# The rounded half of a split piece written by ScalarE from PSUM instead of by VectorE from SBUF

## What is computed

```
# first block (adaLN from a vector c, residuals scaled by alpha = 2 ** 0.25)
u  = layer_norm(x) * (1 + scale1) + shift1
m  = concat(retention_4_heads(u @ w_in), gated_linear_attention_4_heads(u @ w_in)) @ w_out
x  = layer_norm(alpha * x + gate1 * m, ln1_w, ln1_b)
u2 = layer_norm(x) * (1 + scale2) + shift2
x  = layer_norm(alpha * x + gate2 * (square(relu(u2 @ w_ff1)) @ w_ff2), ln2_w, ln2_b)
# second block (mem: 256 rows)
y  = concat(ssd(x @ w_in), s5(x @ w_in), rglru(x @ w_in)) @ w_out
h  = layer_norm(alpha * x + y, ln1_g, ln1_b)
h  = layer_norm(alpha * h + cross_attention(h, mem, wq, wk, wv, wo), ln2_g, ln2_b)
h  = layer_norm(alpha * h + square(relu(h @ w1)) @ w2, ln3_g, ln3_b)
```

## Time and profile before

| | |
|---|---|
| median of three runs | 3189.3 us |
| the three runs | 3180.47, 3189.3, 3190.94 us |
| the profiled execution | 3180.87 us, span 3178.8 us |
| busy: PE | 2748.9 us (86%) |
| busy: DVE | 1526.9 us (48%) |
| busy: ACT | 967.1 us (30%) |
| busy: POOL | 685.1 us (22%) |
| mean granted TensorE clock | 0.931 |

### The profile page before, as it was taken

How to read it: one execution, slowest core, us unless ns; L and a number is a source line. 1 busy time by engine, 2 the same in 40 slices (tenths; PEclk the granted TensorE clock), 3 DMA queues, 4 the chain that set the end, 5 groups by cost and what they waited for, 6 DMA issues and landing times.

```text
span 3178.8 us, 34257 instructions
## 1 busy us (share of the span) xinstructions
PE 2748.9 (86%) x13390; PEld 1408.0 (44%) x13390; DVE 1526.9 (48%) x2347; ACT 967.1 (30%) x1115; POOL 685.1 (22%) x210
## 2 busy tenths in 40 slices
PE   5999958785899999998868785568889999999996
PEld 3577635532444444444454432224444444444443
DVE  6146223357344444456555559965324832222225
ACT  2323212212322222224333253215332422223331
POOL 1211011110122222211522122412511621112224
PEclk8999978887899999999989898878899999999998
DMA  8222030020111111111021220011101021111111
GB/s 276 80 67 67 31 106 27 27 93 1 53 53 53 53 53 53 48 48 38 28 80 66 67 80 0 0 40 38 42 27 40 27 67 39 53 53 53 53 40 53
DMA packets 95643, 172.83 MB, mean 54 GB/s; under 512 B 5648, under 2 KB 37792, under 8 KB 94752
## 3 DMA queue, kind: packets, MB, share of 16 engines
q1 hardware_dynamic: 83232, 134.70, 13.1%
q10 hardware_dynamic: 12288, 36.46, 3.2%
HBM read 164.85 MB, written 6.29 MB: 54 GB/s over the span
## 4 chain that ended last, share of the span: by engine, by line
PE 64%; DVE 15%; DVEq 5%; ACT 4%; issue 4%; POOLq 3%; DMA 1%; PEld 1%; SPq 1%; ACTq 1%; PEldq 0%; POOL 0%
PE PS L585 19%; PE PS L586 19%; PE PS L587 19%; DVEq L1863 2%; DVE XT L1864 1%; ACT WS L1341 1%; PE PS L1274 1%; DVE Hf L1864 1%; DVE S L2552 1%; ACT WB L1340 1%; DVE S L2556 1%; PE PS L624 1%; PE PS L1247 1%; DVEq L2558 1%; DVE ST L1883 1%
## 5 line engine op out<-in xcount | busy, mean ns | idle before, releaser
L480 POOL TENSOR_TENSOR WB<-WS,WB 128x2048 f16<-128x2048 f32 x108 | 448.3, 4171 | 2134.8 <-ACT WS L1341 2134.3
L585 PE MATMUL PS<-XT,WB 128*128 128x512 f16 (+1 forms) x1584 | 605.1, 382 | 33.9 <-DVE Hf L1862 10.8
L586 PE MATMUL PS<-XT,WB 128*128 128x512 f16 (+1 forms) x1584 | 604.5, 382 | 0.0
L587 PE MATMUL PS<-XT,WB 128*128 128x512 f16 (+1 forms) x1584 | 604.2, 381 | 0.0
L585 PE MATMUL PS<-WB,Hf 128*128 128x512 f16 x1440 | 548.7, 381 | 30.8 <-DVE S L2186 9.8
L586 PE MATMUL PS<-WB,Hf 128*128 128x512 f16 x1440 | 548.5, 381 | 0.0
L587 PE MATMUL PS<-WB,Hf 128*128 128x512 f16 x1440 | 548.4, 381 | 0.0
L1862 DVE CAST Hf<-S 128x512 f16<-128x512 f32 x172 | 158.4, 921 | 548.0 <-ACT S L1564 430.9
L1340 ACT ACTIVATE WB<-WS 128x2048 f16<-128x2048 f32 (+3 forms) x118 | 212.5, 1800 | 583.3 <-PEq L594 551.3
L585 PEld LDWEIGHTS PS<-XT,WB 128*128 128x128 f16 (+1 forms) x1584 | 155.6, 98 | 232.9 <-issue 33.0
L2183 DVE SCALAR_TENSOR_TENSOR R<-PS,R 128x512 f32<-128x512 f32 x176 | 120.9, 691 | 263.5 <-PE PS L587 259.7
(11 more groups left out here) (341 smaller groups left out, 3046.5 us busy)
## 6 DMA issues: line engine op xcount, KB each, us to landing
WS<-in_w_ff SPq DMA_DIRECT2D x32, 1024.0 KB, 5.1
WS<-in_mlp_w SPq DMA_DIRECT2D x32, 1024.0 KB, 5.2
WS<-in_w_in SPq DMA_DIRECT2D x48, 256.0 KB, 4.5
Hf<-in_w_ada ACTq DMA_DIRECT2D x12, 1024.0 KB, 7.6
Hf<-in_w_ada SPq DMA_DIRECT2D x8, 1024.0 KB, 10.2
WS<-in_w_out SPq DMA_DIRECT2D x8, 1024.0 KB, 5.0
WS<-in_w_in SPq DMA_DIRECT2D x14, 512.0 KB, 3.9
R<-in_x SPq DMA_DIRECT2D x4, 1024.0 KB, 10.1
```

The costliest lines, as they stand in the source:

```text
L480: pool.tensor_tensor(WB[:, slot, 1, hf * 2048:(hf + 1) * 2048], WS[:, hf, :], WB[:, slot, 0, hf * 2048:(hf + 1) * 2048], ALU.subtract).the ...
L585: pe.matmul(o, ah, bh, start=(first and k == 0), stop=False, skip_group_check=True)
L586: pe.matmul(o, ah, bl, start=False, stop=False, skip_group_check=True)
L587: mm = pe.matmul(o, al, bh, start=False, stop=(last and k == n - 1), skip_group_check=True)
```

## The change

Outside the MLPs' hidden layers and the opening, ACT reads each bank twice with the same function, scale and bias: first into TMP as before, then into the float16 destination, and the second reading frees the bank. DVE no longer casts or drains; it waits for `tmp_full` and for the bank's evacuation, and subtracts. ACT's function `columns_half` gets the number of the half, since it now writes into XT itself. ACT waits for `kv_saved` ahead of the SSD pieces; DVE keeps its own wait. 108 pieces are changed.

```diff
+            def to_pieces(bank, hi, func, scale=1.0, bias=0.0):
+
+                to_tmp(PS[:, bank, :], func, scale, bias).then_inc(tmp_full, 1)
+                act.activation(hi, PS[:, bank, :], func, scale=scale, bias=bias).then_inc(evac[bank], 1)
+
+            def half_of(t, k, hf):
+                return t[:, 0, k, hf * HALF:(hf + 1) * HALF]
...
-            def columns_half(scale, bias):
+            def columns_half(hf, scale, bias):
 
                 for k in range(KT):
                     b = side_in()
-                    to_tmp(PS[:, b, :], ACT.Identity, scale(k), bias(k)).then_inc(tmp_full, 1)
+                    to_pieces(b, half_of(XT, k, hf), ACT.Identity, scale(k), bias(k))
...
             K[0] = SIDE["ssdT"]
+            act.wait_ge(kv_saved, 48)
             for hf in range(2):
                 for k in range(4):
                     b = side_in()
-                    to_tmp(PS[:, b, :], ACT.Copy, col("ssd_norm", k)).then_inc(tmp_full, 1)
+                    to_pieces(b, half_of(H, k, hf), ACT.Copy, col("ssd_norm", k))
...
+            def rest_piece(k, hi, lo):
+
+                q = Q[0]
+                Q[0] += 1
+                dve.wait_ge(tmp_full, q + 1)
+                need_side(dve, k)
+                dve.tensor_tensor(lo, TMP[:, q % 4, :], hi, ALU.subtract).then_inc(piece_done, 1)
...
             def columns_half(hf, dst):
                 for k in range(KT):
-                    b = 4 + K[0] % 4
                     K[0] += 1
-                    split_piece(b, dst[:, 0, k, hf * HALF:(hf + 1) * HALF], dst[:, 1, k, hf * HALF:(hf + 1) * HALF])
+                    rest_piece(K[0] - 1, dst[:, 0, k, hf * HALF:(hf + 1) * HALF], dst[:, 1, k, hf * HALF:(hf + 1) * HALF])
```

More of the change, by code:

```diff
@@ L1456, in _ @@
                         bb = side_in()
-                        to_tmp(PS[:, bb, :], ACT.Copy, col("ret_norm", h)).then_inc(tmp_full, 1)
+                        to_pieces(bb, half_of(H, h, g), ACT.Copy, col("ret_norm", h))
             barrier(2)
@@ L1520, in _ @@
                         b = side_in()
-                        to_tmp(PS[:, b, :], ACT.Copy, col("gla_norm", 2 * pr + hh)).then_inc(tmp_full, 1)
+                        to_pieces(b, half_of(H, 4 + 2 * pr + hh, hf), ACT.Copy, col("gla_norm", 2 * pr + hh))
             barrier(3)
-            def columns_half(scale, bias):
+            def columns_half(hf, scale, bias):
                 for k in range(KT):
                     b = side_in()
-                    to_tmp(PS[:, b, :], ACT.Identity, scale(k), bias(k)).then_inc(tmp_full, 1)
+                    to_pieces(b, half_of(XT, k, hf), ACT.Identity, scale(k), bias(k))
             def load_rows(name, w, bias, at=0):
@@ L1541, in norm_tail @@
                     if t == 3:
-                        columns_half(scale, bias)
+                        columns_half(0, scale, bias)
                 if roots == 2:
                     round_chunk(first + 1)
-                columns_half(scale, bias)
+                columns_half(1, scale, bias)
                 if roots == 1:
@@ L1611, in _ @@
                 b = side_in()
-                to_tmp(PS[:, b, :], ACT.Copy, X_SCALE).then_inc(tmp_full, 1)
+                to_pieces(b, MEMT[:, 0, 2 * q:2 * q + 2, :].rearrange("p k m -> p (k m)"), ACT.Copy, X_SCALE)
             act.activation(AROW, col("a_log", 0, 8), ACT.Exp)
@@ L1828, in _ @@
                         b = side_in()
-                        to_tmp(PS[:, b, :], ACT.Copy, O_SCALE).then_inc(tmp_full, 1)
+                        to_pieces(b, half_of(H, 2 * h + i // 2, i % 2), ACT.Copy, O_SCALE)
             K[0] = SIDE["wo"]
@@ L2071, in _ @@
                 for g in range(2):
-                    b = 4 + ret_side(h, "mt", g) % 4
-                    split_piece(b, H[:, 0, h, g * HALF:(g + 1) * HALF], H[:, 1, h, g * HALF:(g + 1) * HALF])
+                    rest_piece(ret_side(h, "mt", g), H[:, 0, h, g * HALF:(g + 1) * HALF], H[:, 1, h, g * HALF:(g + 1) * HALF])
             barrier(2)
@@ L2144, in _ @@
                     for hf in range(2):
-                        b = 4 + K[0] % 4
                         K[0] += 1
-                        split_piece(b, H[:, 0, 4 + 2 * pr + hh, hf * HALF:(hf + 1) * HALF],
+                        rest_piece(K[0] - 1, H[:, 0, 4 + 2 * pr + hh, hf * HALF:(hf + 1) * HALF],
                                     H[:, 1, 4 + 2 * pr + hh, hf * HALF:(hf + 1) * HALF])
@@ L2285, in _ @@
             for q in range(4):
-                split_piece(4 + (SIDE["mem"] + q) % 4,
+                rest_piece(SIDE["mem"] + q,
                             MEMT[:, 0, 2 * q:2 * q + 2, :].rearrange("p k m -> p (k m)"),
@@ L2413, in _ @@
                 for k in range(4):
-                    split_piece(4 + (SIDE["ssdT"] + 4 * hf + k) % 4, H[:, 0, k, hf * HALF:(hf + 1) * HALF],
+                    rest_piece(SIDE["ssdT"] + 4 * hf + k, H[:, 0, k, hf * HALF:(hf + 1) * HALF],
                                 H[:, 1, k, hf * HALF:(hf + 1) * HALF])
@@ L2620, in _ @@
                 for i in range(4):
-                    b = 4 + att_side(h, "o", i) % 4
                     d, hf = i // 2, i % 2
-                    split_piece(b, H[:, 0, 2 * h + d, hf * HALF:(hf + 1) * HALF],
+                    rest_piece(att_side(h, "o", i), H[:, 0, 2 * h + d, hf * HALF:(hf + 1) * HALF],
                                 H[:, 1, 2 * h + d, hf * HALF:(hf + 1) * HALF])
```

## The result

The changed kernel takes 3203.1 us (median of six runs, 3199.6 to 3204.3), the kernel before, in six runs beside it, 3182.1 us (3180.4 to 3190.9). The ratio is 1.0057, 95% interval 1.0042 to 1.0072: 18 us slower, with 13 to 23 us within the interval. The forecast was 3206 us, the sum of its terms +17 on a median of three runs, 3189.3; on the 3182.1 of six runs the same sum gives 3199. The profiled execution took 3200.1 us with a span of 3198.4, against 3180.9 and 3178.8: +19.6 in the span.

A forecast was written before the change was run, and what follows sets the result against it. DVE set a piece's pace (1.12 us), passing to ACT (1.34). Terms 6.3 + 4.5 + 6.3 + 0.3 + 0.2 - 0.3 - 0.3 = +17 us on the median 3189.3 gave 3206 us, range 3190 to 3220.

The forecast's parts named there:

- The pace of a half: Eight tail pieces: ACT's readings 0.67 us apart set the pace instead of DVE; each first half ends 1.7 us later.
- rival 2: Halves get shorter because two ACT readings take less than DVE's 1.12 us, deciding from spacing 0.56: 3173 us, chance 0.07.
- Second halves: Tails' second eight pieces: ACT is kept 10.72 us, not 6.16, so its next work moves by 4.56 us.
- MLP 1: Tail behind MLP 1: ACT's roundings delay POOL's dt split, for which PE already waits: +6.3 us.
- wo: Tail behind wo: ACT's roundings, POOL's work and the first hidden tile's cast all move: +6.3 us.
- w_out: Tail behind w_out: second half wins 1.4 us, first half loses 1.7: +0.3 us.
- w_out2: Tail behind w_out2: PE's fifth query job starts at 2227.1 instead of 2222.6, waiting for ACT's bank reading: +4.5 us.
- The GLA pair: Ahead of the second GLA pair: PE waits for POOL's split of gla1, so faster casts win little: -0.3 us.
- The memory pieces: Four memory transposes: ACT's extra 2.3 us is covered by its waits for PE: 0.
- Rivals. 1: Second halves absorbed by slack behind ACT, only first halves cost: +5 to +10 us, 3197, chance 0.17.
- 3's price: Rival of a slower kernel: ACT's spacing 0.78 gives +31 us; with 2 for the clock, 3222 us, chance 0.16.
- Its clock half: Same slower rival: PE's clock falls in the longer wait at MLP 2's first hidden tile, adding 2 us.

The follow-up runs named there:

- experiment 6: Kernel before, with ACT writing the rounded half only for odd column blocks in the first half of each tail (16 of 108 pieces): 3179.0 us, ratio 0.9983.
- experiment 7: Changed kernel, with ACT's second reading in the tails a Copy with constant scale, without column scale and bias: 3184.0 us, ratio 0.9997 to the kernel before.
- experiment 1: Kernel before, with the change in mixers, memory pieces, SSD output and attention only (44 of 108 pieces), the four tails unchanged: 3181.4 us, ratio 0.9991.
- experiment 3: Kernel before, with the change only in the four pieces of the first GLA pair, ahead of the second pair: 3180.3 us, ratio 0.9984.
- experiment 8: Three kernels, ratios to before: memory pieces alone changed, 1.0027; changed kernel with memory pieces as before, 1.0031; memory pieces alone, DVE's first convolution awaiting POOL's dt split, 0.9999.
- experiment 4: Kernel before, with the change only in the first half of each of the four tails (32 pieces): 3189.1 us, ratio 1.0024.
- experiment 5: Kernel before, with the change only in the second half of each of the four tails (32 pieces): 3192.5 us, ratio 1.0026.
- experiment 9: The changed kernel measured and traced once more, nothing altered: 3200.5 us, ratio 1.0040 to the kernel before.

## Why the prediction was right, and where it was not

**The pace of a half: right.** The price taken between 0.58 and 0.78 for a second reading of the same bank, 0.67, is 0.663. Row 4 at T + 11.71 (11.67 forecast), +1.7 for each first half. Experiments 6 and 7 move it by what the two paces give, so rival 2's condition, a spacing below 0.56, was put rightly as far as they reach: at (0.67 + 0.47) / 2 = 0.57 row 4 stands at T + 10.25, still 0.28 behind before.

**Second halves: right in what decides, ACT's queue.** MLP 1 by itself is +6.6 (6.3 forecast), though not only by the path that the forecast named (below); wo is +6.1 (6.3). Behind w_out PE restarts at 803.46; the difference goes from -2.85 to -4.30, the 1.4 that the forecast gave back, and of it 0.4 is lost again because the lower clock holds longer behind the restart (5.0 us against 4.2; the earlier trace rows begins 0.24 behind it).

**w_out2: the start right, the size not.** The fifth job starts at 2235.28 and not 2222.6. Less the 8.1 us that the kernel is behind there, that is +4.6 (4.5 forecast), and PE's wait is 2.11. But the term goes on through the first head of the attention: +5.8 here and 6.2 in the second trace, 3.3 in the tails alone and without the memory pieces. In the two traces with 5.8 and 6.2 the clock is at 0.50 for 3.4 us behind that wait, in the two with 3.3 it stays at 1.00; that is 1.7 us of the difference, and the rest is open. The term was 4.5 plus or minus 1.5, a bound the forecast didn't have.

**The GLA pair: the step that failed, -0.3 for -2.7.** The forecast took POOL's work at 514.24 for the split of gla1, on which PE waits. It is the split of out0. That of gla1 stands 92 us earlier, in rows of POOL's timeline of the kernel before that the forecast doesn't show:

```profile
422.17 4.07 POOL L480 TENSOR_TENSOR WB<-WS,WB 128x2048 f16<-128x2048 f32 x1 [81.10 <-ACT WS L1341]
426.64 4.07 POOL L480 TENSOR_TENSOR WB<-WS,WB 128x2048 f16<-128x2048 f32 x1 [0.41 <-ACT WS L1341]
```

The row named what PE had waited for, DVE's cast, and I argued it away with the code. Experiments 1 and 3 settle it.

**The memory pieces: the other step that failed, 0 for +3.4.** I priced the ACT readings and named PE as cover; the price was on DVE's side. Its eight operations beside POOL (1526.16 to 1545.37, 19.2 us) became four (11.0 us), and the convolution moved up beside the residual, for which PE waits. The forecast had "POOL works without a gap ahead of it" in hand and did not ask what an earlier DVE would collide with. Experiment 8 shows this.

**The two errors nearly cancel**, -2.4 and +3.4, and that is luck: it brought the sum close, 17 forecast, 18 and 13 by the two ratios. The 3206 us had luck of its own in a base 7 us above the median of six runs. The retention's -0.8 for -0.3 is small. The steps at 380 to 520 us (-2.3) and 600 to 720 (+1.4) can come without the change: the kernel with first halves alone has nothing changed ahead of 720 us and shows -2.6 and +1.7 there. But the first stands in five of the six traces in which ACT rounds the retention pieces and in one of the seven others, the second in all seven with the first GLA pair by ACT and in two of the six others, so that the change may make either likelier; this is open.

**What the profile was to show.** ACT's sixteen readings over 10.8 us, DVE's subtractions 1.34 apart, PE idle 2 us ahead of the fifth query job, over 6 us at MLP 2 in the first trace: all there. PE's wait for the dt weights was to be 4.7 and is 3.3, though POOL came 8.5 later and not 6.3 (its dt split moves from 1547.65 to 1552.29, and the kernel was 3.9 ahead when the tail began). PE was free for them at 1550.33 and not at 1547.45, with the 3.9 some 6.8 later and not 2.6. It waits for banks of the z product, which ACT reads behind its roundings: this is a wait that the forecast missed. Three rows name it, of the changed kernel (where PE had been at the lower clock from 1491 to 1498 us and had less left to wait), of that without the memory pieces and of the tails alone.

```profile
1506.53 0.38 PE L585 MATMUL PS<-WB,XT 128*128 128x512 f16 x1 [0.60 <-ACT S L1616]
```

```profile
1506.70 0.38 PE L588 MATMUL PS<-WB,XT 128*128 128x512 f16 x1 [3.52 <-ACT S L1624]
```

```profile
1510.31 0.38 PE L588 MATMUL PS<-WB,XT 128*128 128x512 f16 x1 [3.53 <-ACT S L1624]
1555.63 0.17 PE L588 MATMUL PS<-WB,XT 128*128 128x8 f16 x1
```

With the tails alone PE doesn't wait for POOL at all: POOL splits the dt weights at 1553.95, 6.3 later as forecast, and PE takes them at 1555.63 without a gap. There it is PE's own wait for ACT that carries the +6.6, and not "PE waits for POOL already". With both POOL and PE hanging on ACT's queue, the term is as large as forecast all the same; of its mechanism the queue was right and the path was half of it.

**Rivals.** 1 falls with experiments 4 and 5. 2 falls with the spacing. 3's price came from a spacing of 0.78, and it was 0.66. Its clock half is seen and cost nothing at its place: behind the wait of 6.49 at MLP 2 the clock is at 0.50 for 5.8 us and the rows fall 2.5 further behind, but some 10 us later they are back at +19.9.

The Trainium skill, SBUF — State Buffer, section Who interferes with whom, bears on the memory pieces: a VectorE instruction with two SBUF inputs contends with a GpSimd instruction that reads SBUF. The trace agrees, with 3.1 us for POOL's 2.35 and 9.8 us for 4.0 of DVE's scalar_tensor_tensor.

## What to carry to other kernels

Price a piece on both engines and take the slower pace, even where neither is busy for half the span; moving half of the pieces (experiment 6) beat moving none or all. A freed engine doesn't idle: look at what it starts sooner and whom that work slows, here POOL, for which PE waited. Where a row names what an engine waited for, don't overrule it by the code without finding the start of the work that the code names.

## What the runs showed of the hardware

ACT's recorded durations grow within a gapless stream, from 0.78 to 0.87 us over sixteen readings, while the starts stay 0.66 apart: durations overlap, and only the spacing prices a stream. A second reading of the same PSUM bank starts as soon as one of another bank.

How PE's clock falls behind a wait does not follow from the wait's length alone. The same wait ahead of the same job in MLP 2, in the kernel before and in that with the first halves alone:

```profile
2550.91 0.39 PE L585 MATMUL PS<-XT,WB 128*128 128x512 f16 x1 [3.45 <-DVE Hf L1862]
```

```profile
2558.83 0.61 PE L588 MATMUL PS<-XT,WB 128*128 128x512 f16 x1 [3.44 <-DVE Hf L1880]
```

The matmul of 0.39 us runs at 2.4 GHz and the one of 0.61 at 1.2; this costs 2.8 us. Ahead of the fifth query job PE waits 2.11 us in the first trace of the changed kernel and in that of the tails alone; behind it the clock is at 0.50 for 3.4 us in the one and stays at 1.00 in the other. The time thus changed by one to three us at such a wait where a stage had moved by a few us, and also between two traces of one kernel (the barrier, experiment 9). Twice it was more: in the traces of the memory pieces alone and of the second halves alone PE stays at 0.50 from about 614 to 641 us, behind a wait of 2.10 that left it at 1.00 in the kernel before, and the rows behind are 9.4 us or more late. Of the memory pieces alone:

```profile
620.00:630.00 10.00, 10.00 (x45) 7.01 (x42) 3.69 (x23) 0.21 (x1) 0.00 (x0) 0.50 0.01 2
630.00:640.00 10.00, 10.00 (x47) 6.52 (x46) 1.67 (x7) 0.00 (x0) 0.00 (x0) 0.50 0.00 0
```

That is about the distance of the two levels at which the runs of the kernel before lie (3181 and 3190 us). That every run at the upper level has it is likely and was not shown.
